# A hybrid mixer backbone on eight cores: two normalisation tails rewritten as two interleaved streams, with Ln and Exp in place of Sqrt and reciprocal

## The reference, cut to what matters

```python
# mixer B, per head of 64 channels
o = o_fw + flip(o_bw)
o = o * lax.rsqrt(jnp.mean(o * o, axis=-1, keepdims=True) + EPS)
o = o.reshape(B, L, W_B).astype(q.dtype) * norm_g * jax.nn.silu(g_out)
# mixer A, over 256 channels; u is the output of the width-31 convolution
mu = jnp.mean(xf, axis=-1, keepdims=True)
var = jnp.mean(jnp.square(xf - mu), axis=-1, keepdims=True)
layernorm = ((xf - mu) * lax.rsqrt(var + EPS)).astype(x.dtype) * g + b
y_a = jax.nn.silu(layernorm(u)) @ p["w_out_a"]
```

## Time and profile before

| | us |
|---|---|
| median of 2 runs | 3775.04 |
| the two runs | 3614.74 and 3935.34 |
| the profiled execution, its own time | 3614.15 |
| its span on the slowest core (core 2) | 3613.1 |
| spans of the eight cores | 3585.0 to 3613.1 |
| PE busy | 2575.3 (71%) |
| DVE busy | 1771.1 (49%) |
| ACT busy | 991.3 (27%) |

### The profile page before, as it was taken

How to read it: one execution, slowest core, us unless ns; L and a number is a source line. 1 busy time by engine, 2 the same in 40 slices (tenths; PEclk the granted TensorE clock), 3 DMA queues, 4 the chain that set the end, 5 groups by cost and what they waited for, 6 DMA issues and landing times.

```text
span 3613.1 us, 41351 instructions; the slowest of 8 cores (3585.0 to 3613.1 us)
## 1 busy us (share of the span) xinstructions
PE 2575.3 (71%) x12849; PEld 1174.6 (33%) x13048; DVE 1771.1 (49%) x2581; ACT 991.3 (27%) x1831; POOL 427.7 (12%) x433
## 2 busy tenths in 40 slices
PE   0465656825299977999956556593509998699996
PEld 0232332412144423444423333241204443244442
DVE  0466665756455542221245656684665555213224
ACT  0454543220022222101035455323002221210112
POOL 2300000000111032101040000000011102310103
PEclk9855757967599988999966566696859998799997
DMA  9100001704634104333420000100015330343432
GB/s 172 13 4 15 3 4 24 117 0 70 84 31 42 27 1 41 43 36 36 47 22 3 16 2 4 19 7 0 0 14 54 32 38 1 35 46 34 36 44 94
DMA packets 274821, 118.75 MB, mean 33 GB/s; under 512 B 206640, under 2 KB 266288, under 8 KB 274608
## 3 DMA queue, kind: packets, MB, share of 16 engines
q0 software_dynamic: 253584, 95.80, 23.3%
q1 hardware_dynamic: 21024, 20.30, 2.0%
HBM read 201.36 MB, written 10.49 MB: 59 GB/s over the span
## 4 chain that ended last, share of the span: by engine, by line
PE 65%; DVE 15%; issue 7%; ACT 5%; DMA 4%; POOL 3%; DVEq 0%; SPq 0%; ACTq 0%; POOLq 0%; another core or an unknown queue 0%
PE ps L472 34%; PE ps L1234 8%; PE ps L694 5%; PE ps L1187 3%; DMA wp<-ada_w 3%; PE ps L1150 2%; DVE Sbuf L791 2%; DVE khT L760 2%; PE ps L950 2%; PE ps L948 2%; PE ps L952 2%; PE ps L765 1%; PE ps L833 1%; PE ps L827 1%; POOL sq L566 1%
## 5 line engine op out<-in xcount | busy, mean ns | idle before, releaser
L472 PE MATMUL ps<-h,wp 128*128 128x512 bf16 x5648 | 1341.1, 391 | 210.6 <-DVE uc_out L1042 59.1
L472 PEld LDWEIGHTS ps<-h,wp 128*128 128x128 bf16 x5760 | 569.1, 100 | 920.1 <-issue 297.2
L1219 DVE TENSOR_TENSOR act<-ps,sil 128x512 bf16<-128x512 f32 x176 | 121.7, 692 | 513.9 <-PE ps L472 492.0
L1234 PE MATMUL ps<-act,wp 128*128 128x512 bf16 x1380 | 303.1, 379 | 1.5
L1216 ACT ACTIVATE sil<-ps 128x512 f32<-128x512 f32 x176 | 105.2, 598 | 647.3 <-PE ps L472 647.3
L1162 ACT ACTIVATE sg<-ps 128x512 f32<-128x512 f32 x256 | 152.9, 597 | 396.9 <-PE ps L472 385.1
L795 ACT ACTIVATE Sbf<-Sbuf 128x128 bf16<-128x128 f32 x512 | 156.2, 308 | 215.0 <-DVE Sbuf L791 185.2
L765 PE MATMUL ps<-v_tm,khT 128*128 128x128 bf16 x512 | 67.8, 278 | 200.5 <-DVE khT L760 200.4
L694 PE MATMUL ps<-h,wp 128*128 128x512 bf16 x484 | 179.0, 534 | 31.2 <-DVE qp L732 14.3
L1237 DVE SCALAR_TENSOR_TENSOR x<-ps,mod,x 128x512 f32<-128x512 f32 x128 | 96.1, 751 | 208.1 <-PE ps L1234 208.1
L1234 PEld LDWEIGHTS ps<-act,wp 128*128 128x128 bf16 x1408 | 137.7, 98 | 166.2
(11 more groups left out here) (169 smaller groups left out, 3027.7 us busy)
## 6 DMA issues: line engine op xcount, KB each, us to landing
wp<-ada_w POOLq DMA_DIRECT2D x24, 1024.0 KB, 10.0
wp<-ffn_w POOLq DMA_DIRECT2D x88, 256.0 KB, 5.3
wp<-w_in POOLq DMA_DIRECT2D x84, 256.0 KB, 7.0
wp<-ffn_w POOLq DMA_DIRECT2D x16, 704.0 KB, 7.3
x<-xT SPq DMA_DIRECT2D x32, 256.0 KB, 22.3
yT<-ntmp SPq DMA_DIRECT2D x32, 256.0 KB, 2.1
wp<-w_in POOLq DMA_DIRECT2D x4, 1024.0 KB, 8.7
wp<-w_o POOLq DMA_DIRECT2D x4, 1024.0 KB, 8.3
```

What stands on the lines that cost most here:

```text
L472: op("pe", lambda e: e.matmul(ps[bank][0:M, :], lhsT=lhsT, rhs=h[:, kc, g * GT:(g + 1) * GT], start=(kc == 0), stop=(kc == KC - 1)), reads ...
L1219: op("dve", lambda e: e.tensor_tensor(out=act[:, jj, gs], in0=ps[b2][:], in1=st_[:], op=ALU.mult), reads=[("ps", b2), st_.name], writes=[( ...
L1234: op("pe", lambda e: e.matmul(ps[bank][:], lhsT=wt[:, jj * 256 + nn * 128:jj * 256 + nn * 128 + 128], rhs=act[:, jj, gs], start=(jj == 0), ...
```

## The change

Both tails are rewritten as generators for `run_sched`, two streams th each, of which stream 0 takes the groups 0 and 2 and stream 1 the groups 1 and 3. Each tail now has two passes. The first (`post_stat`, `ln_stat`) makes the reciprocal root of all four groups, and keeps each in its own tile. The second (`post_gate`, `ln_apply`) does the gate matmuls, the Silus and the last products. Sqrt and reciprocal become Ln and Exp with scale -0.5, both on ACT. In the LayerNorm tail the bf16 copy of `acc` moves from ACT to DVE.

The core of the diff:

```diff
-                        for g in range(NG):
-                            gs = slice(g * GT, (g + 1) * GT)
-                            op("act", lambda e: e.activation(out=sqb[:], in_=o_acc[:, gs], func=AF.Square),
...
-                            op("act", lambda e: e.activation(out=f_t[:], in_=ps[5][:], func=AF.Sqrt, bias=epsD, scale=1.0 / 64),
-                               reads=[("ps", 5), "mpk"], writes=["f_t"])
-                            op("dve", lambda e: e.reciprocal(out=f_t[:], in_=f_t[:]), reads=["f_t"], writes=["f_t"])
-                            bank = zbank()
-                            zmm(bank, wBb, kB, wg, 128, g)
...
+                        rst = [f_t, k_t, b_t, bq_t]
+                        sqbs = [sqb, khs[0]]
+                        sils = [kp32, e1s[0]]
...
+                        def post_stat(th):
+                            bank = 5 if th == 0 else 6
+                            sq_ = sqbs[th]
+                            for g in (th, th + 2):
...
+                                yield OP("act", lambda e: e.activation(out=sq_[:], in_=o_acc[:, gs], func=AF.Square),
+                                         reads=[("o_acc", g, 0), ("o_acc", g, 1)], writes=[sq_.name])
+                                yield OP("pe", lambda e: e.matmul(ps[bank][:], lhsT=blk_bf, rhs=sq_[:], start=True, stop=True),
+                                         reads=[sq_.name, "cbf"], writes=[("ps", bank)], n=512)
+                                yield OP("act", lambda e: e.activation(out=rg[:], in_=ps[bank][:], func=AF.Ln, bias=epsD, scale=1.0 / 64),
+                                         reads=[("ps", bank), "mpk"], writes=[rgk], aset="lnexp")
+                                yield OP("act", lambda e: e.activation(out=rg[:], in_=rg[:], func=AF.Exp, scale=-0.5),
+                                         reads=[rgk], writes=[rgk], aset="lnexp")
+                                ptok2[g] = yield OP("dve", lambda e: e.tensor_tensor(out=rg[:], in0=rg[:], in1=o_acc[:, gs], op=ALU.mult),
...
+                        def post_gate(th):
+                            bank = th
+                            sl_, slk = sils[th], silk[th]
+                            for g in (th, th + 2):
...
+                                yield from zmm_g(bank, wBb, kB, wg, g)
+                                yield OP("act", lambda e: e.activation(out=sl_[:], in_=ps[bank][:], func=AF.Silu),
+                                         reads=[("ps", bank)], writes=[slk], aset="silu")
+                                yield OP("dve", lambda e: e.scalar_tensor_tensor(out=ob_out[:, p, gs], in0=rg[:], scalar=cp(f"hng{l}", p, 1), in1=sl_[:],
...
+                        run_sched(S, post_stat(0), post_stat(1))
+                        run_sched(S, post_gate(0), post_gate(1))
...
+                    def ln_stat(th):
+                        bs, bq = (4, 5) if th == 0 else (2, 3)
+                        for g in (th, th + 2):
+                            gs = slice(g * GT, (g + 1) * GT)
+                            for ch in range(2):
+                                ab, s2 = accb[th * 2 + ch], sq2[th * 2 + ch]
+                                yield OP("dve", lambda e: e.tensor_copy(out=ab[:], in_=acc[:, ch, gs]), reads=[("acc", ch)], writes=[ab.name])
...
+                            yield OP("act", lambda e: e.activation(out=rg[:], in_=rg[:], func=AF.Ln, bias=epsD, scale=1.0),
+                                     reads=[rg.name, "mpk"], writes=[rg.name], aset="lnexp")
+                            ltok[g] = yield OP("act", lambda e: e.activation(out=rg[:], in_=rg[:], func=AF.Exp, scale=-0.5),
...
+                    def ln_apply(th):
+                        t = tn[th]
+                        for g in (th, th + 2):
...
+                    run_sched(S, ln_stat(0), ln_stat(1))
+                    run_sched(S, ln_apply(0), ln_apply(1))
```

More of the change, by code:

```diff
@@ new lines, in build_program @@
+                    accb = [T(es3, U("accb"), [128, GT], BF16) for _ in range(4)]
+                    sq2 = [T(es3, U("sq2"), [128, GT], BF16) for _ in range(4)]
+                    mean = [T(es3, U("mean"), [128, GT]) for _ in range(NG)]
+                    rstl = [T(es3, U("rstl"), [128, GT]) for _ in range(NG)]
+                    tn = [T(es3, U("tn"), [128, GT]) for _ in range(2)]
+                    ltok = {}
+                    def ln_stat(th):
+                        bs, bq = (4, 5) if th == 0 else (2, 3)
+                        for g in (th, th + 2):
+                            gs = slice(g * GT, (g + 1) * GT)
+                            for ch in range(2):
+                                ab, s2 = accb[th * 2 + ch], sq2[th * 2 + ch]
+                                yield OP("dve", lambda e: e.tensor_copy(out=ab[:], in_=acc[:, ch, gs]), reads=[("acc", ch)], writes=[ab.name])
+                                yield OP("pe", lambda e: e.matmul(ps[bs][:], lhsT=ones_bf, rhs=ab[:], start=(ch == 0), stop=(ch == 1)),
+                                         reads=[ab.name, "cbf"], writes=[("ps", bs)], n=512)
+                                yield OP("act", lambda e: e.activation(out=s2[:], in_=acc[:, ch, gs], func=AF.Square), reads=[("acc", ch)], writes=[s2.name])
+                                yield OP("pe", lambda e: e.matmul(ps[bq][:], lhsT=ones_bf, rhs=s2[:], start=(ch == 0), stop=(ch == 1)),
+                                         reads=[s2.name, "cbf"], writes=[("ps", bq)], n=512)
+                            mg, rg = mean[g], rstl[g]
+                            yield OP("dve", lambda e: e.tensor_scalar(out=mg[:], in0=ps[bs][:], scalar1=1.0 / 256, scalar2=0.0, op0=ALU.mult, op1=ALU.add),
+                                     reads=[("ps", bs)], writes=[mg.name])
+                            yield OP("dve", lambda e: e.tensor_tensor(out=rg[:], in0=mg[:], in1=mg[:], op=ALU.mult), reads=[mg.name], writes=[rg.name])
+                            yield OP("dve", lambda e: e.scalar_tensor_tensor(out=rg[:], in0=ps[bq][:], scalar=1.0 / 256, in1=rg[:],
+                                                                             op0=ALU.mult, op1=ALU.subtract),
+                                     reads=[("ps", bq), rg.name], writes=[rg.name])
+                            yield OP("act", lambda e: e.activation(out=rg[:], in_=rg[:], func=AF.Ln, bias=epsD, scale=1.0),
+                                     reads=[rg.name, "mpk"], writes=[rg.name], aset="lnexp")
+                            ltok[g] = yield OP("act", lambda e: e.activation(out=rg[:], in_=rg[:], func=AF.Exp, scale=-0.5),
+                                               reads=[rg.name], writes=[rg.name], aset="lnexp")
@@ new lines, in ln_apply @@
+                    def ln_apply(th):
+                        t = tn[th]
+                        for g in (th, th + 2):
+                            gs = slice(g * GT, (g + 1) * GT)
+                            mg, rg = mean[g], rstl[g]
+                            for ch in range(2):
+                                yield OP("dve", lambda e: e.tensor_tensor(out=t[:], in0=acc[:, ch, gs], in1=mg[:], op=ALU.subtract),
+                                         reads=[("acc", ch), mg.name], writes=[t.name])
+                                yield OP("dve", lambda e: e.tensor_tensor(out=t[:], in0=t[:], in1=rg[:], op=ALU.mult),
+                                         reads=[t.name, rg.name], writes=[t.name], expect=[(rg.name, ltok[g])])
+                                yield OP("act", lambda e: e.activation(out=ua_out[:, ch, gs], in_=t[:], func=AF.Silu,
+                                                                       bias=cp(f"lab{l}", ch, 1), scale=cp(f"lag{l}", ch, 1)),
+                                         reads=[t.name, "cpk"], writes=[("ua_out", ch, g)], aset="silu")
```

47 lines of the change are left out of this document (9 added, 38 removed).

## The result

The profiled execution of the changed kernel took 3491.68 us, against 3614.15 before: 122.5 us less, where 119.3 were forecast. Over 11 runs the median is 3496.37 us (3488.91 to 3834.86), that of the kernel before, in 10 runs beside it, 3882.74 (3612.56 to 3953.1). Both sets hold executions in which one die was at a lower clock; without them the ratio is 0.9661, with a 95% interval of 0.9642 to 0.9681. That is 3.4% faster; laid on the profiled time of before, 3614.15, it gives 3491.6 us, 3.3 us under the forecast.

A forecast was written before the change was run, and what follows sets the result against it. The tails, 261 us, were taken as bound by a serial chain over four groups. Savings of 73.0 (LayerNorm), 19.9 (HGRN p=0) and 26.4 (HGRN p=1) make 119.3; 3614.15 less that gives 3495 us, range 3478 to 3520.

The forecast's parts named there:

- move along and neither win nor lose: Mixer D: the `ada_w` blocks on the chain (12.46 us) go out when PE has used the block before, costing nothing extra.
- so the slowest stays slowest: Across cores: the other cores have the same tails, so the same core was to remain the slowest.
- six steps of 0.80: LayerNorm tail, statistics rounds: DVE was to make six instructions, 0.80 us from start to start.
- The LayerNorm tail: LayerNorm tail in each layer: 30.6 us instead of 67.06, 36.5 us less, 73.0 in two layers.
- The cast, taken at 0.42 to 0.45: LayerNorm tail, round one: each cast on DVE takes 0.42 to 0.45 us; the slower bound was 0.69.
- The added wait: HGRN tails: all 32 gate matmuls stand behind the last statistic on PE, leaving PE idle 6.3 us in each tail.
- The gates at a rising clock: HGRN tails: the 32 gate matmuls run without a break and reach full clock, 8.8 us, plus some 0.3 for a Silu.
- The rival with the low clock: HGRN tails: gate matmuls stay at 1.2 GHz, 13.8 us instead of 8.8 in four tails, hence 3517; chance 0.09.
- the rival with the reloads: Both tails: Ln and Exp reload the table each time they alternate, 49 us, hence 3544; chance 0.02.
- The rival without overlap: Both tails: the two streams do not overlap, so the gain is 60 us, hence 3554; chance 0.04.
- The dense stretches: Merge and feed-forward, some 1585 us: rival that they lose clock; at 0.89 the kernel takes 3691; chance 0.02.
- The cover of mixer C's weights: Before mixer C: its DMAs land by 724, its start is about 743; the cover shrinks from 56 us to 19 and holds.

## Why the prediction came out as it did

The mechanism of the tails was right: the load pattern, the overlap and the rising clock came as described. Three steps failed.

One is a term put at nothing: the `ada_w` blocks "move along and neither win nor lose". Mixer D of layer 0 became 3.7 us longer in the mean, and 9.7 from the slowest core of before to that of after. The second is "so the slowest stays slowest": it is core 4 now, which gives 11.6 us in the recurrence. The third is a mis-sized term of the sum, "six steps of 0.80": three of the five steps between them measured 0.60, and with the other small differences the six tails lost 127.2 us instead of 119.3.

The sum still comes out 3.2 us from the measured 122.5, and that is luck: 119.3 + 7.9 (tails) + 11.6 (another core) - 9.7 (mixer D) - 6.6 (the rest) = 122.5. It also hangs on the base. The forecast was made against 3614.15, where it is 3.3% less. Against 3775.04, the median printed for before, 3495 would be 7.4% less, more than double the 3.4% that the ratio shows; the choice of the base was right, and was stated.

By its steps, and against what the rows show:

- **The LayerNorm tail: 28.25 and 27.80 us instead of 30.6.** I had read 0.80 from the earlier trace rows at a place where each DVE instruction needs the one before. In two streams three of the five steps within a round don't, and those take 0.60, which is 1.2 us over the two rounds, or 2.4 of the 5.1 that the two tails gained over the walk. Most of the rest is in the apply pass. The first mean starts at 2.05 (2.3 was said), the load at 4.8 (5.5), the mean of group 2 at 10.3 (11.1). The apply round was said to take 3.2 and takes 3.01, the pass 14.0 instead of 14.8. Gain 78.1 instead of 73.0.
- **The cast, taken at 0.42 to 0.45**, is 0.42 (420 ns). By the slower bound, 0.69, the sum would have been off by 1.4 us.
- **The added wait: PE idle for 6.3 us.** Gate matmuls start 6.0 us after time 0 (332.27 - 326.23). The size of the idle time was right. So was its price, 25 us in four tails, as an upper bound: with the gates early the four tails are 18.9 us shorter. The prediction had counted this wait in its sum but not asked whether the change could have done without it.
- **The gates at a rising clock: 8.8 us for 32**, with 0.3 for the Silu in between. Measured: 332.27 to 341.12, 8.85 in all, the wait (0.39) included, and 9.35 in layer 1. The rival with the low clock is out: 3.61 us for the last sixteen is the full clock.
- **No load before Ln, one before the Silus**: so it is, and the rival with the reloads is out.
- **The p=0 stretch** is 22.04 and 22.55 instead of 23.1, **the p=1 tail** 16.60 and 16.75 instead of 17.3. Gain 49.1 together instead of 46.3.
- **The rival without overlap** was put at 3554. The run with one stream after the other took 3543.9, so its price was right to about 10 us, and the changed kernel isn't there.
- **The dense stretches** keep their clock. The first and the last of four, as in the earlier trace rows:

```profile
923.00:1257.00 334.00, 330.14 (x1467) 143.04 (x1495) 180.89 (x256) 78.87 (x131) 38.97 (x51) 1.00 0.30 32
...
2985.00:3442.00 457.00, 452.94 (x2062) 205.90 (x2102) 108.94 (x152) 54.45 (x91) 42.72 (x47) 1.00 0.33 36
```

The granted clock is 1.00 in both, and merge and feed-forward are 0.5 us longer in the mean of the cores. The rule that the prediction set beside this rival, that of the Trainium skill ("TensorE: Matmul & The Clock Gate", the note on the peak-current limiter in Part 1), would have shown 0.81 with eight cores in dense matmuls. The trace after the change doesn't agree either.
- **The cover of mixer C's weights** held: PE starts it 0.25 us after the last Silu and waits for that Silu, not for a DMA.
- **"They move along and neither win nor lose"**, of the `ada_w` blocks, was wrong. The kernel before already waited over 40 us for them, and the eight cores fetch them at about the same time. A stage whose length is set by its fetches needn't keep its length when the stages ahead of it shrink. It cost 3.7 us in the mean and 9.7 from the one slowest core to the other. Of the 3.7, 3.5 go away with the fetches cut (15.6 - 12.1).
- **"The slowest stays slowest"** was wrong. Core 2 was slowest because of mixer B, 7.3 and 5.5 us over the mean of the cores in the two layers. Core 4 is 7.3 over the mean in mixer D of layer 0 and 6.1 in mixer B of layer 1, and 4.1 under it in mixer B of layer 0.

## What to carry to other kernels

A tail of short instructions over a few groups is a chain: take out the longest instruction, put the functions of one table into one pass, and run two groups side by side; where the interleaving puts the long instructions of all groups ahead of the last products of any, the two halves of such a change are worth more together than apart. Where statistics are put ahead of independent matmuls, give the matmuls to the gaps between them, which fills idle time and brings the clock up earlier. And when a kernel gets shorter, look at the next stage that waits for its fetches before calling it unchanged.
